# Summing the later modulation on POOL instead of VectorE in a three-layer fp32 kernel

## The reference

```python
def modulation(cvec, ada_w, ada_b):
    m = jax.nn.silu(cvec) @ ada_w + ada_b
    return jnp.split(m, 3, axis=-1)

def modulate(x, shift, scale):
    return layer_norm(x) * (1.0 + scale) + shift

def post_norm(x, out, gate, g, bias):
    return layer_norm(DEEPNORM_ALPHA * x + gate * out) * g + bias
```

## Time and profile before

| | us |
|---|---|
| median of 3 runs | 3088.56 |
| the runs | 3067.39, 3088.56, 3092.36 |
| the profiled execution's time | 3067.87 |
| its span | 3066.1 |
| PE busy / DVE busy / ACT busy / POOL busy | 2928.7 / 1826.5 / 1309.3 / 189.2 |

### The profile page before, as it was taken

The page is one execution under the profiler, slowest core; times in us unless marked ns, Lnnn a source line. Parts: engine busy times, 40 slices in busy tenths (PEclk is TensorE's granted clock), DMA queues, the critical chain, the costliest instruction groups (busy, mean ns, idle before and its releaser), DMA issues.

```text
span 3066.1 us, 51312 instructions
## 1 busy us (share of the span) xinstructions
PE 2928.7 (96%) x22672; PEld 2729.0 (89%) x22672; DVE 1826.5 (60%) x2112; ACT 1309.3 (43%) x1414; POOL 189.2 (6%) x201
## 2 busy tenths in 40 slices
PE   6999988899899999998999999999999999999998
PEld 2699876679898998898999999998999999999998
DVE  6746765566766644446455454578556766467753
ACT  7723343234634334334343333834434444344444
POOL 0000001000000000000221211002000000000000
PEclk8999998999899999998999999999999999999999
DMA  8745555446476554444444444343044555555554
GB/s 350 295 159 206 206 181 175 139 182 244 145 266 226 197 195 171 146 155 139 170 152 163 153 157 152 127 165 110 4 162 165 193 193 192 197 196 195 192 180 140
DMA packets 90845, 547.10 MB, mean 178 GB/s; under 512 B 10592, under 2 KB 10752, under 8 KB 45696
## 3 DMA queue, kind: packets, MB, share of 16 engines
q1 hardware_dynamic: 69408, 465.86, 42.6%
q0 software_dynamic: 18432, 67.12, 6.1%
q10 hardware_dynamic: 2784, 10.85, 0.9%
HBM read 541.69 MB, written 2.10 MB: 177 GB/s over the span
## 4 chain that ended last, share of the span: by engine, by line
PE 79%; DVE 10%; ACT 4%; issue 3%; DMA 3%; SPq 0%; DVEq 0%; ACTq 0%
PE bank L714 78%; DVE r L2083 3%; ACT r L1421 2%; DMA f<-in_later 2%; DVE f L2117 2%; DMA f<-in_units 1%; PE bank L776 1%; PE bank L1045 0%; DVE f L2263 0%; DVE f L2636 0%; ACT f L1754 0%; DVE f L2633 0%; DVE f L2136 0%; DVE f L2572 0%; DVE f L2649 0%
## 5 line engine op out<-in xcount | busy, mean ns | idle before, releaser
L714 PE MATMUL bank<-r,r 128*128 128x256 f32 (+3 forms) x19888 | 2496.9, 287 | 52.6 <-DVE r L2083 28.7
L714 PEld LDWEIGHTS bank<-r,r 128*128 128x128 f32 (+2 forms) x19888 | 2374.0, 188 | 167.1 <-issue 76.4
L2083 DVE TENSOR_TENSOR r<-f,r 128x2048 fp32r<-128x2048 f32 (+3 forms) x478 | 1031.8, 2161 | 848.9 <-ACT r L1421 847.0
L1421 ACT CAST r<-f 128x2048 fp32r<-128x2048 f32 (+3 forms) x478 | 852.6, 1786 | 916.8 <-PE bank L714 762.6
L714 PE MATMUL bank<-f,f 128*128 128x128 f32 (+15 forms) x2334 | 432.7, 329 | 47.2 <-DVE f L2123 9.6
L714 PEld LDWEIGHTS bank<-f,f 128*128 128x128 f32 (+6 forms) x2334 | 314.7, 190 | 102.2 <-issue 36.3
L2117 DVE SCALAR_TENSOR_TENSOR f<-f,f,f 128x512 f32<-128x512 f32 x240 | 179.9, 750 | 41.4 <-DMA f<-in_later 33.4
L2572 DVE SCALAR_TENSOR_TENSOR f<-f,f,f 128x255 f32<-128x255 f32 (+1 forms) x272 | 132.5, 489 | 8.8
L1438 ACT COPY f<-bank 128x512 f32<-128x512 f32 (+2 forms) x141 | 80.8, 590 | 117.3 <-PE bank L714 112.3
L2902 POOL DMA_DIRECT2D f<-in_later x128 | 68.0, 531 | 963.2 <-DVE f L2117 784.8
L1587 ACT ACTIVATE f<-bank,f 128x512 f32<-128x512 f32 x32 | 22.0, 688 | 137.7 <-DVE f L2270 131.1
(11 more groups left out here) (219 smaller groups left out, 878.2 us busy)
## 6 DMA issues: line engine op xcount, KB each, us to landing
f<-in_units SPq DMA_DIRECT2D x346, 1024.0 KB, 4.8
f<-in_units SPq DMA_DIRECT2D x120, 768.0 KB, 4.3
f<-in_later POOLq DMA_DIRECT2D x128, 512.0 KB, 5.0
f<-in_units SPq DMA_DIRECT2D x8, 576.0 KB, 4.4
f<-in_x ACTq DMA_DIRECT2D x2, 1024.0 KB, 12.8
f<-in_ctx ACTq DMA_DIRECT2D x2, 1024.0 KB, 11.3
f<-in_x_turned ACTq DMA_DIRECT2D x1, 2048.0 KB, 14.2
f<-in_units SPq DMA_DIRECT2D x2, 800.0 KB, 4.4
```

The costliest lines, as they stand in the source:

```text
L714: return e.matmul(o, lhsT, rhs, start=start, stop=stop, skip_group_check=True)
L1421: e.copy(unit_view(high[HIGH_OF[u]][1], u), unit_view(raw[RAW_OF[u]][0], u)).then_inc(*up("w_hi", ("hi", u)))
L2083: e.tensor_tensor(unit_view(raw[RAW_OF[u]][1], u), unit_view(raw[RAW_OF[u]][0], u), unit_view(high[HIGH_OF[u]][1], u).bitcast(F32), ALU.su ...
```

## The change

The 128 steps leave DVE and go to POOL, which already issues their transfers. [...] The first tile of a block is multiplied straight into the accumulator. A step is so 4 instructions instead of 2 (3 in a block's first), and behind each step POOL issues the transfer of the step after next. `plan_later` and its dealing out are gone. The blocks' ends on PE, and DVE's addition of the bias, stand behind 16 fixed units: 50, 55, 60, 64, 69, 73, 76, 80, 83, 86, 91, 98, 112, 118, 124, 130. Before, they stood behind 49, 53, 57, 62, 68, 73, 77, 80, 83, 86, 92, 97, 118, 126, 134, 142.

```diff
-LATER_STEPS, LATER_ENDS = plan_later()
+LATER_ENDS = {u: [n] for n, u in enumerate((50, 55, 60, 64, 69, 73, 76, 80, 83, 86, 91, 98, 112, 118, 124, 130))}
+assert LIN["ckv"].us[3] < 50 and LIN[("oA", 0)].us[0] == 85 and LIN[("oF", 0, 0)].us[0] > 130
...
         def dve_after(e, u):
-            for n in LATER_STEPS.get(u, []):
-                dve_later(e, n)
             for blk in LATER_ENDS.get(u, []):
                 dve_later_end(e, blk)
...
-        def dve_later(e, n):
-            o = acc[(n // 8) % 2]
-            e.wait_ge(*at("own landed", n))
-            for kt in range(2):
-                w, s = own[:, n % 2, kt, :], cv[:, 2 * (n % 8) + kt, 0:1]
-                if n % 8 + kt == 0:
-                    e.wait_ge(*(at("ps", "later", n // 8 - 2) if n >= 16 else at("cv")))
-                    ins = e.tensor_scalar(o, w, s, None, ALU.mult)
-                else:
-                    e.wait_ge(*now("dve_ada"))
-                    ins = e.scalar_tensor_tensor(o, w, s, o, ALU.mult, ALU.add)
-                ins.then_inc(*up("dve_ada", ("later summed", n)))
...
+        def pool_own(e, n):
+            e.dma_start(own[:, n % 2, :, :], a["later"][n // 8, n % 8].rearrange("p (k c) -> p k c", k=2)).then_inc(
+                *up(f"own_half{n % 2}", ("own landed", n), by=16))
+
+        def pool_later(e, n):
+
+            o = acc[(n // 8) % 2]
+            e.wait_ge(*at("own landed", n))
+            for kt in range(2):
+                w, s = own[:, n % 2, kt, :], cv[:, 2 * (n % 8) + kt, 0:1]
+                if n % 8 + kt == 0:
+                    if n >= 16:
+                        e.wait_ge(*at("ps", "later", n // 8 - 2))
+                    e.tensor_scalar(o, w, s, None, ALU.mult).then_inc(*up("pool_ada", ("later summed", n)))
+                else:
+                    e.tensor_scalar(w, w, s, None, ALU.mult).then_inc(*up("pool_ada"))
+                    e.wait_ge(*now("pool_ada"))
+                    e.tensor_tensor(o, o, w, ALU.add).then_inc(*up("pool_ada", ("later summed", n)))
+
         def gpsimd_program(e):
+            e.wait_ge(*at("cv"))
+            e.wait_ge(*at("used", max(u for u in range(len(HEAD) - 4) if RAW_OF[u] == 5)))
+            pool_own(e, 0)
+            pool_own(e, 1)
             for n in range(128):
-                if n > 1:
-                    e.wait_ge(*at("later summed", n - 2))
-                else:
-                    e.wait_ge(*at("used", max(u for u in range(len(HEAD) - 4) if RAW_OF[u] == 5)))
-                e.dma_start(own[:, n % 2, :, :], a["later"][n // 8, n % 8].rearrange("p (k c) -> p k c", k=2)).then_inc(
-                    *up(f"own_half{n % 2}", ("own landed", n), by=16))
+                pool_later(e, n)
+                if n + 2 < 128:
+                    e.wait_ge(*at("later summed", n))
+                    pool_own(e, n + 2)
```

## The result

The changed kernel takes **3275.6 us** (median of four runs, 3275.2 to 3302.3) against 3078.9 us of the kernel before (four runs, 3067.4 to 3092.4). The ratio is 1.066, with a 95% interval from 1.058 to 1.074. I had forecast 3049 us, a range of 3012 to 3110, and 0.20 for slower by over 1%. The time lies outside the range, and the rival that I had at 0.20, POOL as the bound, is what happened, by more than its own upper figure.

The account below looks back on a forecast made before the run. PE bounds the kernel, waiting for DVE's sums in the first stretch (ceiling 49 us); POOL would finish at 734 us instead of 752, so 3067.9 - 18 = 3050, less 1 for the second stretch: 3049 us, range 3012 to 3110.

Parts of the forecast that it names:

- POOL as the bound: Rival, chance 0.20: block 11's sum ends late if a multiplication exceeds 0.71 us; 3098 us at 0.90, 3157 at 1.27.
- The price of a multiplication: POOL's multiplication of 512 columns by a scalar: 0.60 us, between bounds of 0.54 and 1.27; 0.67 with the gap.
- A transfer: POOL's issue of a transfer: 0.72 us, 0.79 with the wait on the addition ahead; eight in a block.
- The gaps: Between a POOL instruction and one that waits for it: 0.07 us, added to each multiplication and addition.
- The start of block 2 at 270 us: POOL, having summed blocks 0 and 1, may start block 2 when PE ends unit 50, at about 270 us.
- Hindrance: DVE's two-input work stops POOL's calculations in the first stretch: 93 us over the ten blocks 2 to 11.
- POOL's end of block 11: First stretch: start at 270, ten blocks 371 us, hindrance 93 us, so POOL is done at 734 us.
- Block 14 has 66 us for its 37 and a third of that more: no wait: Second stretch: 12 units from 112 to 124, some 66 us, suffice for POOL's block 14, so PE doesn't wait.
- The second stretch: 813 to 1052 us, PE nearly always busy: 3 us to win at most, 1 us counted; blocks 12 and 13 cost nothing.
- the forecast's 18 us: Gain in the first stretch: POOL ends block 11 at 734 us against 752 before, leaving 18 of the 49 us.
- PE's waits for POOL: At the blocks' ends from block 6 on, 2 to 7 us each; over 8 us at most ends would mean slower.
- The ceiling of 49 us: First stretch: PE's idle time and lost clock, 72.5 us, less 23.2 us of softmax waits, the most to be gained.

Follow-up runs that it names:

- e4: The kernel before with nine forms of POOL's work, four times each, ahead of its first transfer; multiplication of 128x512 by a column of scalars took 1.56 us.
- e9: The changed kernel with POOL's multiplications L2875 over 128 of 512 columns (0.61 us each): 3083 us, 1.003 of the kernel before.
- e5: The changed kernel with the blocks' ends behind the units of the kernel before: 3246 us, 1.056 of the kernel before.
- e6: The changed kernel with its last 32 steps given back to DVE, at the ends of the kernel before: 3235 us, 1.053 of the kernel before.
- e10: The kernel before with POOL summing only the last four blocks, product by a repeated column: 3087 us, 1.004 of the kernel before.
- e1: The changed kernel without POOL's multiplications L2875 (15 of a block's 16): 3050 us, 0.987 of the kernel before.
- e2: The changed kernel with POOL's multiplications L2875 over 256 of 512 columns (0.93 us each): 3141 us, 1.017 of the kernel before.

## Why the prediction was wrong, step by step

The mechanism, POOL as what PE waits for at the blocks' ends, was in the forecast. What failed was a term of its sum.

- **The price of a multiplication: this step failed.** "With one stream in and one out it is nearer the memset; I take 0.60" stood between bounds of 0.54 and 1.27; it is 1.56, 2.6 times the term and outside both. The bounds rested on an idea of cost by streams that no row had tested. e4 refutes it: one tensor in takes longer than two. Over ten blocks it is 160 x (1.57 - 0.60) = 155 us.
- A transfer costs POOL 0.95 us, not 0.79: 0.60, 0.30 ahead of it for its own addition's signal (37.1 us in 125 waits) and 0.05 behind. 80 x 0.16 = 13 us.
- The gaps were taken as 0.07 us behind each of 31 instructions; they are 0.08 behind the 15 multiplications that an addition waits for and nothing elsewhere: -8 us over ten blocks, with the additions' 1.285 for 1.27.
- The start of block 2 at 270 us assumed that PE holds POOL back. By the price of their own multiplications the first two blocks took until 298, and block 2 began at 299.1: 29 us.
- Hindrance was put at 9.3 us a block. Over the ten blocks 2 to 11 it was 7.2 in the changed kernel (60.4 - 53.2), and what the calculations of these blocks took beyond their undisturbed times was 8.5 in e9. Right in size, -21 us over ten blocks. Counting L2272 to what hinders was right as well: its mean went from 0.49 to 0.73 us.
- Together 734 + 155 + 13 - 8 + 29 - 21 = 902 us for POOL's end of block 11; the trace has 903.5. PE goes on behind unit 98 at 903.6, where it was through with that unit at 751.6 before: 152 of the 207 us. Of the other 55, by the ends of the low parts, some 13 are lost up to unit 112 and some 41 between units 112 and 142, where the two late ends stand.
- "Block 14 has 66 us for its 37 and a third of that more: no wait" failed by the same price, and by block 13, which lay in the crowded units and was done only at 1045.0, 30 us behind unit 112. From there POOL's last additions for blocks 14 and 15 came 65.4 and 62.4 us apart, and PE waited 36.5 us for them. e5 and e6 put the ends' places at 30 to 40 us.
- The second stretch was said to hold nothing but a gain of 1 us: "In the second stretch blocks 12 and 13 fall into the norm" put their cost at nothing without a reason. In these units, 100 to 112, the old plan kept DVE free of sums, and POOL's work beside DVE's costs 17 us in e9 and 22 in e10. By e9 this term alone would have undone nearly all of the forecast's 18 us, had the multiplication cost its 0.60.
- DVE's busy time fell by 118 us (1826.5 to 1708.9), not 180: the low parts alone rose from 1031.8 to 1052.1 us over the span. In the first stretch the mean of those of 2048 columns went from 2.28 to 2.49 us, just under the "over 2.5" foreseen.
- PE's waits for POOL were foreseen from block 6 on at 2 to 7 us; there were ten of 12.5 to 31 us, from the third block on, which is the sign of being wrong that the prediction had named (over 8 us at most ends). The ceiling of 49 us can't be tested directly; e1, without 15 of a block's 16 multiplications, gained 1.35% of 3088, some 40 us.
- The rival "POOL becomes the bound" had the mechanism. Its threshold of 0.71 us was too high: e9 at 0.61 is level with the kernel before or slightly above (1.000 to 1.007), where the formula had it 16 us faster, and e2 at 0.93 is slower. By its formula a multiplication of 1.57 gives 3068 + 160 x 0.86 = 3206 us. What it lacked is in the points above: the later start of block 2, the transfers, and most of all the second stretch.

Of the two places of the Trainium skill that the prediction weighed in advance: DVE's multiplication of 128x512 by a column takes 0.48 us (L2114 before), POOL's 1.56, a factor of 3.2. The Trainium skill (GPSIMD Engine Reference, Engine selection) says of POOL's elementwise work that it is about two times slower with two inputs and "1-input is roughly line-rate"; the second half does not hold for this form, and the measurement decides. Its advice against such a move was right, and I should have let it count for more than 0.20. Its figure of 769 ns for 512 elements fits none of the forms of e4.

## What to carry to other kernels

A price without a row is not bounded by rows of other forms: a multiplication by a scalar cost POOL more than an addition of two tensors, and by the prediction's own sum the sign of the result turned on 0.1 us of it. When work moves to an engine that then runs it at its own pace, compare that engine's time for a unit of work with the bound engine's time for the same unit first, with the price at its worst, and look at which stretches the old plan had left free on purpose. Moving elementwise work from DVE to POOL frees DVE of less than it seems (here 118 us of the 188 that its sums took), because instructions of the one stop those of the other.

## What the runs showed of the hardware

- POOL, fp32, 128x512, undisturbed (e4): store 0.52 us, copy 0.61, product with a repeated column 1.04, addition of two tensors 1.28, tensor and constant 1.49, tensor and column of scalars 1.56. The last takes 0.93 for 256 columns and 0.61 for 128, the addition 0.72 to 0.74 for 256. Why one tensor with a scalar is slower than two tensors stays open; only that it is was measured.
- Writing the same product with two tensors, the second a repeated column, saved the changed kernel some 105 us (3276 to 3171).
- An instruction of POOL that starts during a low part of DVE does nearly all of its work behind it, with one input as with two: it ended behind the low part by its own time less some 0.14 us (0.47 us for the copy of 0.61, 0.59 for an addition of 0.74, 1.43 for the multiplication of 1.56). The other way round a DVE instruction of 0.68 us grew to 1.28 on average beside a busy POOL (e10).
